# Strassen's seven products for the last eight gate tiles and the mixing projection of a two-layer mixer network

## What the reference computes, as far as it matters

```python
h = rmsnorm(x, norm_mix[l])
(u_ssm, q_lat, kv_lat, k_rope, hg_q, hg_f, hg_i, hg_g, gate_logits) = jnp.split(h @ w_in[l], split_at, axis=-1)
...                                            # three mixers: y_ssm, y_mla, y_hg
gates = jax.nn.sigmoid(gate_logits).reshape(bsz, s, 3, D_MODEL)
merged = gates[:, :, 0] * y_ssm + gates[:, :, 1] * y_mla + gates[:, :, 2] * y_hg
x = x + merged @ w_out[l]
x = x + memory_cross_attention(rmsnorm(x, norm_cross[l]), rmsnorm(mem, norm_mem[l]), ...)
x = x + swiglu_ffn(rmsnorm(x, norm_ffn[l]), ffn_w_gate_up[l], ffn_w_down[l])
```

## Time and profile before

| | us |
|---|---|
| median of 3 runs | 1622.03 (1621.83 to 1623.67) |
| the profiled execution's own time | 1623.35 |
| its span in the trace | 1621.5 |
| TensorE busy | 1591.0 (98% of the span) |
| VectorE busy | 875.2 (54%) |
| ScalarE busy | 421.9 (26%) |
| granted TensorE clock, mean | 0.994 of full |

### The profile page before, as it was taken

One profiled execution on the slowest core, in us unless ns is written; L12 is line 12 of the kernel. 1 busy time (PEld: TensorE's weight loads), 2 busy tenths in 40 slices (PEclk: granted clock), 3 DMA queues, 4 the chain that ended last, 5 costly groups with the idle time before them and its releaser, 6 DMA issues.

```text
span 1621.5 us, 25335 instructions
## 1 busy us (share of the span) xinstructions
PE 1591.0 (98%) x10313; PEld 1363.5 (84%) x10313; DVE 875.2 (54%) x1697; ACT 421.9 (26%) x887; POOL 10.4 (1%) x24
## 2 busy tenths in 40 slices
PE   7999999999999999999999999999999999999998
PEld 6778867888899999878877888799999767678887
DVE  4546792223566774446793222567765464435553
ACT  4234423202210001434423201300001344421322
POOL 0100000000000000100000000000000000000000
PEclk9999999999999999999999999999999999999999
DMA  9343252441485455333342432485535815463320
GB/s 312 132 149 112 91 170 80 156 156 53 165 287 172 144 162 191 131 106 112 135 152 83 147 121 96 156 260 175 176 126 200 275 62 207 170 238 111 106 104 27
DMA packets 172374, 243.48 MB, mean 150 GB/s; under 512 B 16830, under 2 KB 95204, under 8 KB 172260
## 3 DMA queue, kind: packets, MB, share of 16 engines
q1 hardware_dynamic: 171204, 239.76, 44.0%
q10 hardware_dynamic: 1056, 2.10, 0.4%
HBM read 240.79 MB, written 1.05 MB: 149 GB/s over the span
## 4 chain that ended last, share of the span: by engine, by line
PE 94%; issue 2%; DVE 1%; ACT 1%; SPq 0%; DMA 0%; POOL 0%; DVEq 0%; ACTq 0%; POOLq 0%
PE psum L602 43%; PE psum L1411 26%; PE psum L613 4%; PE psum L2566 3%; PE psum L414 2%; PE psum L1187 2%; PE psum L2662 1%; PE psum L2670 1%; PE psum L447 1%; PE psum L430 1%; PE psum L1265 1%; PE psum L1237 1%; PE psum L2523 1%; PE psum L636 1%; PE psum L2494 1%
## 5 line engine op out<-in xcount | busy, mean ns | idle before, releaser
L602 PE MATMUL psum<-hT,ring 128*128 128x256 f32 x2448 | 543.5, 381 | 3.7 <-ACT hT L2763 2.6
L602 PEld LDWEIGHTS psum<-hT,ring 128*128 128x128 f32 x2448 | 462.7, 191 | 76.7 <-issue 15.6
L602 PE MATMUL psum<-uT,ring 128*128 128x256 f32 x384 | 85.6, 381 | 0.0
L1411 PE MATMUL psum<-hT,ring 128*128 128x128 f32 x704 | 82.4, 275 | 2.7 <-issue 2.7
L1411 PEld LDWEIGHTS psum<-hT,ring 128*128 128x128 f32 x704 | 80.4, 192 | 3.2 <-issue 3.2
L602 PEld LDWEIGHTS psum<-uT,ring 128*128 128x128 f32 x384 | 72.5, 190 | 10.9 <-issue 0.7
L485 DVE TENSOR_TENSOR psum<-psum,const 128x512 f32<-128x512 f32 (+3 forms) x43 | 22.3, 541 | 106.9 <-PE psum L414 101.5
L1667 ACT ACTIVATE SCR<-SCR 128x512 f32<-128x512 f32 x22 | 13.9, 630 | 221.2 <-DVEq L2168 221.2
L463 ACT ACTIVATE SCR<-psum,stats 128x128 f32<-128x128 f32 (+2 forms) x128 | 49.7, 399 | 74.9 <-DVE stats L499 71.3
L1928 DVE COPY_PREDICATED SCR<-levels,psum 128x512 f32<-128x512 uint8 x32 | 23.4, 733 | 56.7 <-PE psum L1187 56.0
L1443 ACT ACTIVATE G<-psum 128x512 f32<-128x512 f32 x32 | 19.1, 597 | 127.1 <-PE psum L602 127.1
(11 more groups left out here) (507 smaller groups left out, 2562.2 us busy)
## 6 DMA issues: line engine op xcount, KB each, us to landing
ring<-in_w_in SPq DMA_DIRECT2D x46, 1024.0 KB, 7.3
ring<-in_ffn_w_gate_up SPq DMA_DIRECT2D x88, 512.0 KB, 5.9
ring<-in_w_ada SPq DMA_DIRECT2D x24, 1024.0 KB, 10.4
ring<-in_ffn_w_down SPq DMA_DIRECT2D x16, 1024.0 KB, 7.6
ring<-in_w_in_odd SPq DMA_DIRECT2D x16, 1024.0 KB, 7.5
ring<-in_w_in_even SPq DMA_DIRECT2D x10, 1024.0 KB, 7.3
ring<-in_x_w_kv SPq DMA_DIRECT2D x8, 1024.0 KB, 6.2
ring<-in_ssm_w_glu SPq DMA_DIRECT2D x8, 1024.0 KB, 6.9
```

The source lines that it names most:

```text
L602: ins = nc.tensor.matmul(b[0:width, n * S:n * S + S], w[k // 4][:, k % 4, c0[n]:c0[n] + width], tile(k), start=k == 0, stop=k == kt - 1)
L1411: ins = nc.tensor.matmul(banks[job][:, at:at + P], left, right, start=first, stop=last)
```

## The change

The last eight gate tiles become two units `G0`, `G1` and the mixing projection two units `M0`, `M1` of each layer. A unit computes a weight block of 1024 by 512 times the 1024 by 256 tokens. The contraction is cut in halves (tiles 0 to 3 and 4 to 7), the tokens in halves of 128, and the four output tiles into two pairs, and seven products of halves take the place of eight. Each product is 8 matmuls of 128 columns (2 output tiles by 4 tiles of contraction). The products are done in jobs `a` (products 1 and 2), `b` (6 and 5), `c` (7 and 4) and `d` (3). Products 5, 6, 7 and 3 need sums of weights 0 to 3, products 5, 6, 7 and 4 need sums of tokens 0 to 3; VectorE makes them all, and adds the products up. Sum of weights 2 is written over a quarter in the ring's slot, and sum 3 into the place of sum 0, after job `b`. Job `d` of each unit is read by VectorE only.

The four sums of tokens of the gates and the first weight sums of `G0` are made before and during step 0 of the attention. `norm_memory` moves from behind the merging to in front of it, and behind it, also in front of the merging, stand the first three sums of weights of `M0`. The squares are added up on TensorE with six matmuls by ones in place of four. The diff, cut to its core:

```diff
-MLA_FILL = {0: ["gate8"], 1: ["gate9"], 2: ["gate10"], 3: ["gate11"], 4: ["glu gate0"], 5: ["glu out0"]}
+MLA_FILL = {0: ["G0 a", "G0 b"], 1: ["G0 c", "G0 d"], 2: ["G1 a", "G1 b"], 3: ["G1 c", "G1 d"], 4: ["glu gate0"], 5: ["glu out0"]}
...
-    names += [f"mix out{c}" for c in range(4)]
+    names += [f"M{u} {x}" for u in range(MIX_UNITS) for x in "abcd"]
...
-    for n in range(4, 6):
-        wide(f"gate{n}", w_in, OFF_GATE + 512 * n, 512, f"gate{2 * n + 1}")
+    for n in range(GATE_UNITS):
+        for h in range(2):
+            piece(f"gate{4 + n}.{h}", w_in, 4 * h, 4, OFF_GATE + 512 * (4 + n), 512, f"G{n} {'cd'[h]}")
     for n in range(2):
         piece(f"glu gate.{n}", a["ssm_w_glu"], 0, 4, 1024 + 512 * n, 512, f"glu gate{2 * n + 1}")
         piece(f"glu out.{n}", a["ssm_w_glu"], 0, 4, 512 * n, 512, f"glu out{2 * n + 1}")
         piece(f"mla out.{n}", a["mla_w_o"], 0, 4, 512 * n, 512, f"mla out{2 * n + 1}")
         piece(f"hgrn out.{n}", a["hg_w_o"], 0, 4, 512 * n, 512, f"hgrn out{2 * n + 1}")
-    for n in range(2):
-        wide(f"mix{n}", a["w_out"], 512 * n, 512, f"mix out{2 * n + 1}")
+    for n in range(MIX_UNITS):
+        for h in range(2):
+            piece(f"mix{n}.{h}", a["w_out"], 4 * h, 4, 512 * n, 512, f"M{n} {'cd'[h]}")
...
+    def gate_quarters(eng, u):
+        key = f"gate{4 + u}" if u < GATE_UNITS else f"mix{u - GATE_UNITS}"
+        w = [ring.arrived(eng, f"{key}.{h}").rearrange("p k (g m n) -> p k g m n", g=2, m=2) for h in range(2)]
+        return [[w[half][:, :, :, m_, :] for half in range(2)] for m_ in range(2)]
+    def gate_sums(eng, u):
+        if u < GATE_UNITS:
+            first = vx[:, :, :].rearrange("p t (k g n) -> p (t k) g n", g=2, n=P)
+            second = cT[:, 0:2].rearrange("p c a b -> p (c a b)").rearrange("p (k g n) -> p k g n", g=2, n=P)
+        else:
+            first, second = (SCR[:, 2560 + 1024 * i:3584 + 1024 * i].rearrange("p (k g n) -> p k g n", g=2, n=P)
+                             for i in range(2))
+        return [first, second, gate_quarters(eng, u)[1][0], first]
...
+        def gate_job(name):
+            mix, job = name[0] == "M", name[-1]
+            u = int(name[1]) + (GATE_UNITS if mix else 0)
+            b = jobs.begin(pe, name)
+            q, made, mixed_tokens = gate_quarters(pe, u), gate_sums(pe, u), mix_mixed if mix else gate_mixed
+            for i, p in enumerate(PRODUCTS[job]):
+                if p in MIXED_OF:
+                    pe.wait_ge(sig["tokens_mixed"], 4 * mix + MIXED_OF[p] + 1)
+                elif mix:
+                    pe.wait_ge(sig["merged"], 2 * TOKENS_OF[p][0] + 2)
+                if p in SUM_OF:
+                    pe.wait_ge(sig["weights_mixed"], 4 * u + SUM_OF[p] + 1)
+                for g in range(2):
+                    for k in range(4):
+                        if p in WEIGHTS_OF:
+                            m_, half = WEIGHTS_OF[p]
+                            weights = q[m_][half][:, k, g, :]
+                        else:
+                            weights = made[SUM_OF[p]][:, k, g, :]
+                        if p in TOKENS_OF:
+                            half, n = TOKENS_OF[p]
+                            tokens = hT[:, 4 * half + k, n * P:(n + 1) * P]
+                        else:
+                            tokens = mixed_tokens[MIXED_OF[p]][:, k, :]
+                        at = S * i + P * g
+                        ins = nc.tensor.matmul(b[:, at:at + P], weights, tokens, start=k == 0, stop=k == 3)
+            close(ins)
...
-        sum_squares_after("square xc", sq, sig["squares"], 4, sig["summed"], 2, [
-            lambda c=c: transposed(f"mix out{c}", [f"mix{c // 2}.0", f"mix{c // 2}.1"], pair(c), hT, KT,
-                                   wait_tile=lambda k: pe.wait_ge(sig["merged"], k // 2 + 1)) for c in range(4)],
-                          lambda: half_vx("vx0 left"))
+        for u in range(MIX_UNITS):
+            for job in "abcd":
+                gate_job(f"M{u} {job}")
+        b = ojobs.begin(pe, "square xc")
+        half_vx("vx0 left")
+        pe.wait_ge(sig["summed"], 2)
+        for k in (0, 1, 4, 5, 6, 7):
+            if k in (4, 6):
+                pe.wait_ge(sig["squares"], 4 + k // 2 + 1)
+            ins = nc.tensor.matmul(b[:, 0:S], ones, sq[:, k, :], start=k == 0, stop=k == 7)
+        ins.then_inc(o_done, 1)
...
-                if name.startswith("gate"):
-                    gate_copy(int(name[4:]))
-        jobs.evacuated(act, "gate11")
+                if name.endswith(" a"):
+                    u = int(name[1])
+                    b = jobs.full(act, name)
+                    if u:
+                        jobs.evacuated(act, f"G{u - 1} b")
+                    nc.scalar.activation(gate_one, b[:, 0:S], ACT.Copy).then_inc(sig["parts_copied"], 1)
+        jobs.evacuated(act, "gate7")
         for n in range(3):
+            if n == 2:
+                act.wait_ge(sig["gates_made"], GATE_UNITS)
             g = gates[:, 8 * n:8 * n + 8, :]
             nc.scalar.activation(g, g, ACT.Sigmoid)
         for c in range(4):
@@ -1619,7 +1693,16 @@
             if c >= 2:
                 act.wait_ge(sig["glu_mixed"], c - 1)
             jobs.release(nc.scalar.activation(sg[c % 2], b, ACT.Sigmoid), f"glu gate{c}")
-        squares("mix out")
+        for u in range(MIX_UNITS):
+            b = jobs.full(act, f"M{u} a")
+            jobs.evacuated(act, f"M{u - 1} b" if u else f"G{GATE_UNITS - 1} b")
+            nc.scalar.activation(gate_one, b[:, 0:S], ACT.Copy).then_inc(sig["parts_copied"], 1)
+            if u == 0:
+                link(approximate_root(nc, m["warm"], m["eps"], 1, m["eps"]))
+            act.wait_ge(sig["mix_added"], u + 1)
+            for c in (2 * u, 2 * u + 1):
+                nc.scalar.activation(sq[:, 2 * c:2 * c + 2, :], xT[:, 2 * c:2 * c + 2, :],
+                                     ACT.Square).then_inc(sig["squares"], 1)
...
+        def sum_gates(u, which):
+            q, made = gate_quarters(dve, u), gate_sums(dve, u)
+            for i in which:
+                x, y, op = ((q[1][0], q[1][1], ALU.add), (made[0], q[0][0], ALU.subtract),
+                            (q[0][0], q[1][0], ALU.subtract), (q[0][1], made[1], ALU.subtract))[i]
+                link(V.tensor_tensor(made[i], x, y, op))
+                dve.sem_inc(sig["weights_mixed"], 1)
+        def mix_gate_tokens(which, to=gate_mixed):
+            t = [[hT[:, 4 * half:4 * half + 4, n * P:(n + 1) * P] for n in range(2)] for half in range(2)]
+            operands = ((t[0][1], t[0][0]), (t[1][1], to[0]), (t[1][1], t[0][1]), (t[1][0], to[1]))
+            for i in which:
+                link(V.tensor_tensor(to[i], *operands[i], ALU.subtract))
+                dve.sem_inc(sig["tokens_mixed"], 1)
+        def gate_store(name):
+            u, job = int(name[1]), name[-1]
+            made = gates[:, 16 + 4 * u:20 + 4 * u, :].rearrange("p (g m) (n t) -> p g m n t", m=2, n=2)
+            b = jobs.full(dve, name)
+            first, second = b[:, 0:S], b[:, S:2 * S]
+            def put(m_, n, x, y):
+                return V.tensor_tensor(made[:, :, m_, n, :], x.rearrange("p (g t) -> p g t", g=2),
+                                       y.rearrange("p (g t) -> p g t", g=2), ALU.add)
+            if job == "a":
+                dve.wait_ge(sig["parts_copied"], u + 1)
+                jobs.release(put(0, 0, gate_one, second), name)
+            elif job == "b":
+                link(V.tensor_tensor(gate_two, gate_one, first, ALU.add))
+                jobs.release(V.tensor_tensor(gate_four, gate_two, second, ALU.add), name)
+                sum_gates(u, (3,))
+                jobs.evacuated(dve, name)
+            elif job == "c":
+                put(1, 1, gate_four, first)
+                link(V.tensor_tensor(gate_three, gate_two, first, ALU.add))
+                jobs.release(put(1, 0, gate_three, second), name)
+            else:
+                jobs.release(put(0, 1, gate_four, first), name)
+                for x in "acd":
+                    jobs.evacuated(dve, f"G{u} {x}")
+                dve.sem_inc(sig["gates_made"], 1)
+                if u + 1 < GATE_UNITS:
+                    sum_gates(u + 1, (0, 1, 2))
         if layer == 0:
             dve.wait_ge(sig["rope_tables"], 1)
         rope("krope swap", krope.unsqueeze(1))
@@ -2042,8 +2176,18 @@
         ssm_store(1)
         ojobs.evacuated(dve, "ssm out 1")
         dve.sem_inc(sig["y_ready"], 1)
+        mix_gate_tokens((0, 1))
+        sum_gates(0, (0, 1))
         for i in range(mla.steps):
             mla.dve(nc, dve, link, i)
+            if i == 0:
+                mix_gate_tokens((2, 3))
+                sum_gates(0, (2,))
+            for name in MLA_FILL.get(i, []):
+                if name.startswith("G"):
+                    gate_store(name)
+        norm_memory(lambda k: memN[:, k, :], layer, sig["mem_normed"])
+        sum_gates(GATE_UNITS, (0, 1, 2))
 
         for c in range(4):
```

(55 more changed lines are left out.)

## The result

The changed kernel takes 1632.15 us (median of 4 runs, 1630.63 to 1633.17), the kernel before beside it 1622.51. The ratio is 1.0055, with a 95% interval of 1.0042 to 1.0068: slower by 9.6 us. 1630.0 had been forecast. The profiled execution took 1630.63 us with a span of 1628.8, 7.3 us more than before.

The account below looks back on a forecast made before the run. TensorE, 94% of the span, was taken to bound the kernel. Per layer -2.6 - 2.6 + 0.9 + 6.8 + 1.5 = +4.0 us, +8.0 for two, gave 1631.4 profiled, 1630.0 median; range 1625.5 to 1635.

Parts of the forecast that it names:

- The matmuls: TensorE's gates and mixing: 1.31 us saved per unit, 2.6 us per layer for the gates and 2.6 for the mixing.
- outside chance: Weight loads in the units: 48 more loads cost some 9 us per unit, losing about 74 us; chance under 1 in 100.
- The squares: Mixing's sum of squares on TensorE: two more matmuls by ones, four records, cost 0.9 us per layer.
- VectorE in the attention: Attention steps 0 to 3: VectorE busy 28 of 33 us, cost 0, up to 1 us per step if work lumps.
- rival (c): Attention: VectorE also holds it by 1 us in each of four steps, 8 us more, 1638; chance 0.08.
- The standstill: Before `hgrn out1`: TensorE stands 6.8 us per layer while VectorE awaits a mixing weight load, landing at 311.1, then sums.
- (a): Merging: VectorE is not held or the bank comes free otherwise; whole gain of 8.7 us stands, 1613.3; chance 0.06.
- (d): Before `hgrn out1`: the standstill is shorter by about half, as TensorE arrives late otherwise; near 1622; chance 0.05.
- The clock: Behind the standstill: TensorE's granted clock falls to the lower level, costing 1.5 us per layer, bounds 0 and 3.0.
- Rival (b): Behind the standstill: the standstill comes but the clock does not fall; +2.5 us per layer, 1627.0; chance 0.12.
- Mixing: Mixing units: finer waits of the new jobs are all met, three by 0.1 to 0.3 us; 0, up to 0.6 per layer.

Follow-up runs that it names:

- e2: As e1, but VectorE still waits idle in front of the merging for the loads of the first mixing unit's weights; 1622.73 us, 1.0001 of the kernel before.
- e3: As e1, but VectorE does three unused additions of 1024 columns on present data in front of the merging; 1614.16 us, 0.9951 of the kernel before.
- e4: Changed kernel with M0's first two weight loads four pieces earlier in the ring's order, VectorE's order unchanged; 1614.23 us, 0.9948 of the kernel before.
- e1: Changed kernel with M0's first three sums of weights moved from before the merging to behind its c = 1; 1614.94 us, 0.9952 of the kernel before.
- e7: Changed kernel with only the gates in seven products, the mixing as in the kernel before; 1618.28 us, 0.9972 of the kernel before.
- e8: Changed kernel with only the mixing in seven products, its sums placed as in e1, gates as in the kernel before; 1621.69 us, 0.9993 of the kernel before.
- e5: Changed kernel with three more unused additions of 1024 columns behind the three sums in front of the merging; 1638.71 us, 1.0101 of the kernel before.
- e6: As e1, but the mixing's squares are summed with four matmuls instead of six, after one VectorE addition; 1614.05 us, 0.9947 of the kernel before.

## Why the prediction was right

**The matmuls.** `mla out1` starts at 305.77 in place of 308.55, 2.8 us earlier, 0.15 of it from before the attention (247.25 to 247.40): the gates save 2.6 us per layer, as forecast. The outside chance that every added weight load would stand alone is out too: `G1 a` and `G1 b` start at 264.13 and 267.70, 32 records in 3.57 us, the pace of the feed-forward unit. The mixing saves 27.63 - (374.34 - 348.82) = 2.1 us, where 2.6 had been put. The squares cost 0.86 us, as put.

**VectorE in the attention.** It was put at 28 us busy of 33 and is busy 24.16 of 33.05, and TensorE does not wait; the cost of 0 holds, and rival (c) is out. That estimate was too high, and nothing hung on it. The gaps behind eight sums, 0.14 us each, had been counted as busy; the old work had been scaled up with the length of the steps, to 12 us, while its own instructions add up to 10.8; the last addition falls behind the stretch; and records of neighbouring instructions overlap by 1.3 us in all.

**The standstill.** Landing forecast at 311.1, the first sum starts at 311.20; release forecast at 316.2, TensorE starts at 316.13; 6.8 us forecast, 6.75 and 6.62 measured. e2, e3 and e4 show that its cause is the late load and not the sums or their place as such. Rivals (a) and (d) are out with it.

**The clock.** The 16 records behind the standstill take 321.19 - 316.13 = 5.06 us; the same number at full clock takes 3.45 (308.55 to 312.00): 1.6 us, where 1.5 had been put. Rival (b) is out for this standstill. There was some luck in it: at the wait that the 1.5 was read from, the profiled executions of other kernels lost up to 3.0 us or nothing (see the last section). The bounds of the prediction, 0 and 3.0, are the better description.

**Mixing.** The term that was mis-sized. The finer waits were put at 0, bound 0.6; they cost 0.5 us per layer, 25.5 us against 25.0. The places are those that the prediction found met by 0.1 to 0.3 us: `M0 b` starts 3.69 us behind `M0 a`, `M1 b` 3.84 us behind `M1 a`, where 3.57 is the pace of two products. For `M1 b` the timeline of VectorE shows the second sum:

```profile
363.91 1.23 DVE L2127 TENSOR_TENSOR SCR<-SCR,ring 128x1024 f32<-128x1024 f32 x1
```

It ends at 365.14, `M1 b` starts at 365.34, and at the pace of the matmuls it would start at 365.07. The prediction had left out two things here: an idle 0.41 us of VectorE in front of the first sum, and the hop of the semaphore to TensorE, which it counted in the standstill. No run removes these waits, so that they are the whole 0.5 us is read from the trace and not tested.

**Sum.** From start to start the standstill counts 6.9 us (`hgrn out1` would start 3.45 us behind 305.77 and starts at 316.13). Layer 0: -2.8 - 2.1 + 0.9 + 6.9 + 1.6 = +4.5 us, and `xq0` starts at 383.84 in place of 379.34. Two layers make 9 us, where 8 had been put, and the medians differ by 9.6; the last 0.6 us lie within the interval. The profiled executions differ by 7.3 only, because in the one of before the clock also fell once in the second block. The timeline of the kernel before and of the changed kernel at the same place, and then the two stretches:

```profile
1407.81 7.11 PE L2566 MATMUL psum<-memT,ring 128*128 128x256 f32 x24 [0.81 <-ACT SCR L463]
```

```profile
1416.74 5.42 PE L2743 MATMUL psum<-memT,ring 128*128 128x256 f32 x24 [0.69 <-ACT SCR L463]
```

```profile
1407.80:1410.00 2.20, 2.19 (x6) 1.82 (x7) 0.28 (x1) 0.56 (x2) 0.00 (x0) 0.58 1.04 388
```

```profile
1416.70:1419.00 2.30, 2.26 (x11) 2.03 (x12) 0.43 (x2) 0.71 (x2) 0.00 (x0) 1.00 1.04 386
```

The same 24 records behind a wait of 0.8 and 0.7 us: the clock is 0.58 in the one and full in the other, 1.7 us apart. With that, 9.0 - 1.7 = 7.3.

## What to carry to other kernels

Where an engine takes its instructions in order, a wait for a load belongs to everything behind it: before work is moved forward into "idle" time, look up when its operands land, and which bank release stands behind it. A ring's order says when a piece can land at the earliest, and it is as good a place for the mend as the engine's order (e4 and e1 are 0.7 us apart, and their intervals overlap). Seven products for eight are worth 9.5% of the matmul time at 128 columns here; that is 10 us of 1622, less 1.7 for the squares, which one wait of 6.8 us per layer more than eats.

## What the runs showed of the hardware

The lower clock has a price of its own. Behind standstills of 6.75 and of 10.49 us it was the same, 1.5 to 1.6 us. It is not a constant, though. Every kernel has the wait at 53 us that the prediction read the earlier trace rows. In e1 it lasts 4.18 us, and these are the timeline of TensorE and, under it, a stretch behind it:

```profile
53.34 16.96 PE L602 MATMUL psum<-QK,ring 128*128 128x256 f32 x64 [4.18 <-DVE QK L1813]
```

```profile
57.00:58.00 1.00, 1.00 (x4) 0.82 (x3) 0.90 (x4) 0.00 (x0) 0.00 (x0) 0.50 0.00 0
```

The clock is still 0.50 at 57 to 58 us, where it was full in the kernel before. From these 64 records to the next group it is 16.80 us, against 15.34 in the kernel before and 13.82 at full clock: 3.0 us lost in the one, 1.5 in the other. In e2, e7 and e8 2.8 to 3.0 us are lost there, in e4, e5 and e6, where the wait is shorter, nothing or nearly nothing. What makes the difference between 1.5 and 3.0 is open; it is not the length of the wait alone, as 3.0 us went behind 3.56 us (e8) and 1.5 behind 3.70 (before).

Whether the clock falls: it was low behind all four standstills of 6.6 to 10.5 us and behind all seven waits of 3.2 to 4.3 us at 53 us. Behind shorter waits, in places where it had been full, it is open, and the length alone does not decide: it stayed full behind 1.61 us (e6), 1.69 (e7), 2.33 (e4), 2.48 (e5) and 2.59 us (e2, layer 0), and fell behind 0.81 us (before), 1.01 (e6), 1.60 (e8) and 2.38 us (e2, layer 1).

Between two profiled executions this alone can make up to 3 us, so a difference of a few us between two profiles is to be split by place before it is explained.
